# Expert stage by phases: a tile's u dot products first, then its v rows gathered by token

## What is computed

```python
q = (hb @ w_q).reshape(PEER_BLOCK, PEER_HEADS, 2, PEER_QDIM // 2)
s = jnp.einsum('nhpd,pkd->nhpk', q, sub_keys)
s_half, i_half = lax.top_k(s, PEER_TOPK)
cand = (s_half[:, :, 0, :, None] + s_half[:, :, 1, None, :]).reshape(PEER_BLOCK, PEER_HEADS, PEER_TOPK * PEER_TOPK)
cid = (i_half[:, :, 0, :, None] * PEER_NKEYS + i_half[:, :, 1, None, :]).reshape(cand.shape)
best_s, best_j = lax.top_k(cand, PEER_TOPK)
eid = jnp.take_along_axis(cid, best_j, axis=-1)
gate = jax.nn.softmax(best_s, axis=-1)
act = jax.nn.gelu(jnp.einsum('nd,nhkd->nhk', hb, u_tab[eid]))
out = jnp.einsum('nhk,nhkd->nd', gate * act, v_tab[eid])
```

## Time and profile before

| | us |
|---|---|
| median of 3 runs | 3094.18 |
| the runs | 3093.94, 3094.18, 3095.62 |
| span of the profiled execution, first to last instruction | 3089.7 |
| busy: PE, PEld | 2489.5, 1527.7 |
| busy: DVE, ACT, POOL | 1279.6, 386.2, 647.1 |
| expert stage, from the first gather's issue to the end | 1699.3 to 3089.7 |
| bytes read from HBM | 842.46 MB |
| of these gathers of POOL's queue | 586.10 MB |

### The profile page before, as it was taken

How to read it: one execution, slowest core, us unless ns; L and a number is a source line. 1 busy time by engine, 2 the same in 40 slices (tenths; PEclk the granted TensorE clock), 3 DMA queues, 4 the chain that set the end, 5 groups by cost and what they waited for, 6 DMA issues and landing times.

```text
span 3089.7 us, 33087 instructions
## 1 busy us (share of the span) xinstructions
PE 2489.5 (81%) x11463; PEld 1527.7 (49%) x11463; DVE 1279.6 (41%) x2256; ACT 386.2 (12%) x946; POOL 647.1 (21%) x736
## 2 busy tenths in 40 slices
PE   6888879999988688969997676777776777777776
PEld 5665658888877374338786222232322222222222
DVE  3213121003255562210147556555554555555554
ACT  1212120001131141110113000000000000000000
POOL 1000000000000123230000434344432343333332
PEclk9999999999988678979998998999999899999998
DMA  9999985444130263566420999999998799999997
GB/s 296 322 331 322 336 259 186 143 156 141 55 109 1 62 214 119 155 205 206 130 89 1 409 420 366 422 422 422 422 422 346 293 421 422 422 422 422 422 422 303
DMA packets 328937, 852.32 MB, mean 276 GB/s; under 512 B 21246, under 2 KB 232754, under 8 KB 260554
## 3 DMA queue, kind: packets, MB, share of 16 engines
q0 software_dynamic: 84000, 586.10, 46.7%
q1 hardware_dynamic: 240370, 259.48, 26.8%
q10 hardware_dynamic: 4476, 5.58, 0.6%
HBM read 842.46 MB, written 17.21 MB: 278 GB/s over the span
## 4 chain that ended last, share of the span: by engine, by line
PE 46%; DMA 28%; issue 10%; SPq 6%; DVE 5%; POOL 2%; ACT 2%; POOLq 0%; DVEq 0%; PEldq 0%; ACTq 0%
DMA sb_ring<-in_peer_u_dram,sb_work 24%; PE ps L539 12%; PE ps L2196 7%; DMA sb_ring<-in_w_ada_dram 4%; PE ps L1841 4%; PE ps L1730 4%; PE ps L1644 3%; PE ps L362 3%; SPq L200 2%; SPq L199 2%; PE ps L345 2%; POOL sb_ring L2066 2%; PE ps L1629 1%; PE ps L2216 1%; PE ps L1088 1%
## 5 line engine op out<-in xcount | busy, mean ns | idle before, releaser
L2196 PE MATMUL ps<-sb_ring,sb_levels 128*128 128x512 f32 x2048 | 956.5, 612 | 342.3 <-DVE sb_levels L2141 328.9
L2196 PEld LDWEIGHTS ps<-sb_ring,sb_levels 128*128 128x128 f32 x2048 | 375.1, 192 | 924.5 <-DVE sb_levels L2141 474.6
L2099 DVE SCALAR_TENSOR_TENSOR sb_pT<-sb_ring,sb_pT 128x2048 f32<-128x2048 f32 x256 | 586.8, 2292 | 502.2 <-DMA sb_ring<-in_peer_u_dram,sb_work 501.9
L2066 POOL DMA_INDIRECT sb_ring<-in_peer_v_dram,sb_work x256 | 252.2, 985 | 633.3 <-DVE sb_pT L2099 519.9
L539 PE MATMUL ps<-sb_hT,sb_ring 128*128 128x264 f32 x1664 | 370.8, 386 | 0.0
L539 PEld LDWEIGHTS ps<-sb_hT,sb_ring 128*128 128x128 f32 x1664 | 316.0, 190 | 54.4 <-issue 0.4
L2064 POOL DMA_INDIRECT sb_ring<-in_peer_u_dram,sb_work x256 | 270.2, 1055 | 136.7 <-issue 79.4
L2172 ACT ACTIVATE sb_small<-sb_small 128x1 f32<-128x1 f32 x256 | 51.9, 203 | 1224.0 <-DVE sb_pT L2099 1224.0
L987 POOL DMA_DIRECT2D out_conv_p_dram<-sb_work x1 | 0.7, 740 | 694.0 <-DVE sb_work L682 694.0
L345 PE MATMUL ps<-sb_ring,sb_work 128*32 128x256 f32 x1536 | 103.9, 416 | 27.5 <-DMA sb_ring<-in_w_ada_dram 27.5
L2141 DVE TENSOR_SCALAR sb_levels<-sb_ident,sb_small,sb_work 128x128 f32<-128x128 f32 x256 | 95.5, 373 | 69.5 <-ACT sb_small L2172 69.5
(11 more groups left out here) (533 smaller groups left out, 2308.9 us busy)
## 6 DMA issues: line engine op xcount, KB each, us to landing
sb_ring<-in_w_ada_dram SPq DMA_DIRECT2D x48, 2048.0 KB, 17.6
sb_ring<-in_w_in_dram SPq DMA_DIRECT2D x26, 2048.0 KB, 8.4
sb_ring<-in_cache_cmp_kv_dram SPq DMA_DIRECT2D x128, 256.0 KB, 3.3
sb_ring<-in_w_out_dram SPq DMA_DIRECT2D x8, 2048.0 KB, 9.8
sb_ring<-in_peer_wq_dram SPq DMA_DIRECT2D x8, 2048.0 KB, 8.3
sb_ring<-in_cache_sel_kv_dram SPq DMA_DIRECT2D x120, 128.0 KB, 2.9
sb_ring<-in_cache_sel_kv_dram POOLq DMA_DIRECT2D x116, 128.0 KB, 2.9
sb_ring<-in_state_win_kv_dram SPq DMA_DIRECT2D x4, 2048.0 KB, 22.7
```

The lines of the kernel that those rows point to most:

```text
L2066: pool.indirect_dma_start(vbuf[n0 % 4], None, io["peer_v"][0], bass.IndirectOffsetOnAxis(index, 0)).then_inc(v_in[n0 % 4], 16)
L2099: dve.scalar_tensor_tensor(products, ubuf[j], 1.0, h2, ALU.mult, ALU.mult, accum_out=dots[:, column:column + 1]).then_inc(sem("dot"), 1)
L2196: mm = pe.matmul(bank(bk + q), diag[:, n0 % 4, :], vbuf[n0 % 4][:, 512 * q:512 * q + 512], start=False, stop=False)
```

## The change

The expert stage is written anew; the picks are moved.

- **Order of gathers.** One list, `ENTRIES`, has all gathers: tile 0's 128 u gathers (one per slot), then its 128 v gathers (now one per token: the token's 128 slots on the partitions), then 8 u and 8 v gathers for the samples (u by head, v by head, with a sample's 16 slots of a head on 16 partitions), then tile 1's u and v. POOL walks the list without a loop.
- **Buffers.** All eight halves of the ring serve u and v in turn; a gather waits until the one that held its buffer has been used. The first 24 gathers use only four of them, in ring slots 0 and 1 of the four, and may begin while the query projection runs; the query weights use the other two slots only, head by head, so a load waits for the head two before it.
- **Picks head by head.** `dve_head` does one head of one tile to the end, the expert numbers included. In the query projection only tile 0's heads are picked, and after each head from the second on DVE does three dots of gathers that have been issued for the heads before. Key scores of a head are formed half a head earlier (after the first of the next head's two blocks). Tile 1's and the samples' picks follow in `dve_others`, after tile 0's last dot.
- **u phase.** The dots are done slot by slot as before, but in place (the product overwrites the row), with no gelu and no diagonal between them. After the last, ACT applies gelu to the 128 x 128 results at once and DVE multiplies with the gates.
- **v phase.** PE transposes the expert numbers (for the gathers) and the weights. For token n the weight column stands in a 128 x 32 block that is zero but for its own column (`wexp`: a cleared buffer in which ACT writes every 33rd column), and four products with 32 weight columns and 512 row columns put the four quarters of the token's sum on four groups of 32 partitions of one PSUM bank. 32 tokens fill a bank, two banks alternate, ACT moves them to rows (`whole`; for the last group DVE moves two of the four quarters). For the samples a head's 8 samples are one such product set, with `wexp_s`.
- **End of a tile.** The add, the norm and the scale are as before, but those of tile 0 and of the samples stand between tile 1's first dots; SP stores the results.

```diff
@@ sp_out
-            sp_project(sp, G_OUT + 8, 68, 8, io["peer_wq"][0], 0)
+            for h in range(HEADS):
+                sp.wait_ge(sem("proj_sum"), 8 + 52 + 2 * (4 + h + 1) if h < 2 else 8 + 68 + 2 * (h - 1))
+                sp.dma_start(ring[:, wq_slot(h), :].rearrange("p (k n) -> p k n", k=KD), item_src(io["peer_wq"][0], 256 * h)).then_inc(full[wq_slot(h)], 16)
...
+        ENTRIES = [("u", 0, n) for n in range(SLOTS)] + [("v", 0, n) for n in range(P)]
+        ENTRIES += [("u", NT, h) for h in range(HEADS)] + [("v", NT, h) for h in range(HEADS)]
+        ENTRIES += [("u", 1, n) for n in range(SLOTS)] + [("v", 1, n) for n in range(P)]
+        EARLY, PER_HEAD = 24, 3
+        NBUF = 2 * RING
+        rbuf = [ring[:, j // 2, (j % 2) * D:(j % 2 + 1) * D] for j in range(NBUF)]
+        buf_of = lambda e: e % 4 if e < EARLY else (e - EARLY + 4) % NBUF
...
@@ pe_queries
-                if h:
-                    scores(h - 1)
+                    if c == 0 and h:
+                        scores(h - 1)
                 rows(3 * h + 2)
...
@@ dve_queries
-            for h in range(HEADS):
-                dve.wait_ge(sem("keyscores"), h + 1)
-                best(P, range(NT), h, lambda t, half: ks[h % 2][:, t, half])
...
+            for h in range(HEADS):
+                dve.wait_ge(sem("keyscores"), h + 1)
+                dve_head(dve, P, 0, h, [ks0[h % 2][:, half] for half in range(2)])
+                if h:
+                    dve_dots(dve, 0, PER_HEAD * (h - 1), PER_HEAD * h)
+            dve_differences(dve, 0)
+
+        def dve_dots(dve, t, n0, n1):
+            for n in range(n0, n1):
+                rows, here, count = rows_at("u", t, n)
...
+                dve.wait_ge(here, count)
+                dve.scalar_tensor_tensor(rows, rows, 1.0, h2r[:, t, :] if t < NT else h2w, ALU.mult, ALU.mult,
+                                         accum_out=(dots if t < NT else dots_s)[:, n:n + 1]).then_inc(sem("dot"), 1)
...
+        def dve_experts(dve):
+            c = sem("dve_steps")
+            dve_dots(dve, 0, PER_HEAD * (HEADS - 1), 72)
+            dve_gates(dve, 0)
+            dve_ids(dve, 0)
+            dve_dots(dve, 0, 72, SLOTS)
+            dve_weights(dve, 0)
+            dve_others(dve)
+            dve_dots(dve, NT, 0, HEADS)
...
+            dve_add(dve, 0)
+            dve_dots(dve, 1, 0, 4)
+            dve_scale(dve, 0)
+            dve_dots(dve, 1, 4, 12)
+            dve_add(dve, NT)
+            dve_dots(dve, 1, 12, 16)
+            dve_scale(dve, NT)
+            dve_dots(dve, 1, 16, SLOTS)
+            dve_weights(dve, 1)
...
+        def pe_sums(pe, t, n0, n1):
+            for n in range(n0, n1):
...
+                w = wexp[G % 2][:, 32 * j:32 * j + 32] if t < NT else wexp_s[:, j, :]
+                pe.wait_ge(here, count)
+                for q in range(4):
+                    mm = pe.matmul(bank(G % 2)[32 * q:32 * q + 32, :], w, rows[:, 512 * q:512 * q + 512], start=j == 0, stop=j == last)
+                mm.then_inc(sem("v_used"), 1)
...
+        def pe_experts(pe):
+            pe_side(pe)
+            pe.wait_ge(sem("h2_wide"), 4)
+            pe_ids(pe, 0)
+            pe_weights(pe, 0)
+            pe_sums(pe, 0, 0, 44)
+            pe.wait_ge(sem("ids_ready"), 1)
+            pe_ids(pe, 1)
+            pe.wait_ge(sem("found_ready"), 1)
...
+            pe_sums(pe, 0, 44, P)
+            pe_sums(pe, NT, 0, HEADS)
+            pe_weights(pe, 1)
+            pe_sums(pe, 1, 0, P)
...
@@ pool_gather
-            pool.wait_ge(sem("proj_sum"), 8 + 84)
...
-                pool.wait_ge(sem("experts_ready"), t + 1)
...
+            pool.wait_ge(sem("proj_sum"), 8 + 68)
+            last = {}
+            for e, (kind, t, n) in enumerate(ENTRIES):
+                if e == EARLY:
+                    pool.wait_ge(sem("proj_sum"), 8 + 84)
...
+                b = buf_of(e)
+                if b in last:
+                    pool.wait_ge(sem("dot" if ENTRIES[last[b]][0] == "u" else "v_used"), done_of(last[b]))
+                last[b] = e
...
+                pool.indirect_dma_start(rbuf[b], None, io["peer_u" if kind == "u" else "peer_v"][0], bass.IndirectOffsetOnAxis(index, 0)
+                                        ).then_inc(row_in[b], 16)
```

More of the change, by code:

```diff
@@ L2036, in layer_program @@
-        vbuf = [ring[:, 2 + j // 2, (j % 2) * D:(j % 2 + 1) * D] for j in range(4)]
-        v_in = [sem(f"v_in{j}") for j in range(4)]
-        SEQ = (0, NT, 1)
-        FIRST = {0: 0, NT: SLOTS, 1: SLOTS + NB}
-        place = SEQ.index
-        def each_slot(eng, t, body, head=None, turns=(0, HEADS // 2)):
-            with eng.Fori(*turns) as i:
-                for half in range(2):
-                    if head:
-                        head(i, half)
-                    for s in range(TOPK):
-                        body(i, half, s, FIRST[t] + half * TOPK + s)
@@ L2247, in _ @@
             leave(sp, "sp_left")
-            for stage in (sp_w2, sp_states_stored, sp_samp, sp_out):
+            for stage in (sp_w2, sp_states_stored, sp_samp, sp_out, sp_results):
                 stage(sp)
```

567 lines of the change are left out of this document (289 added, 278 removed).

## The result

The changed kernel takes 2987.33 us (median of 4 runs, 2984.48 to 2987.95) against 3094.06 us for the kernel before (4 runs): ratio 0.9658, 95% interval 0.9642 to 0.9673, 107 us less. The forecast was 2972 us, range 2954 to 3035: the sign and most of the size are right, and 15 us of the gain are missing. The profiled execution has a span of 2985.6 us, where the sum made 2967.

The account below looks back on a forecast made before the run. Gathers from HBM were taken to bound the last 1390 us. Savings of 54.7, 21.8, 51 and 4.3 us less 10 make 122 us: span 2967, median forecast 2972 us, range 2954 to 3035.

Parts of the forecast that it names:

- Start of the stream: Query projection: 22 gathers leave the stream (54.7 us), which starts at 1677.5 and not at 1699.3 (21.8 us).
- No hole around the samples: Expert stage: eight buffers cover phase changes and tile 1's selection, so the 51 us lost inside the stage go.
- Dots against gather issue: U phases: DVE's dots hold back POOL's gathers, 2.52 us a row, a cost of 10 us.
- the loop: U phases with three gathers in flight: issue, landing and dot take 2.56 us a row.
- the shut-out by a pile: Start of tile 1's u phase: piled-up rows may keep POOL from issuing, 14 us once, counted in the range only.
- Tail: After the last byte: shorter PE work and fewer copies, 4.3 us less, 20.0 us in all.
- Sum: Whole span: start, latency, 506 transfers, 10 us for dots and the tail make 2967 us; 4.5 more for the median.
- the loop's term: U phases: the 10 us added to the stream for dots and gather issue delaying each other.
- The dots do not pace the u phases: Rival for the u phases: dots and POOL delay each other, 2.79 us a row, 71 us more, 3043; 13%.
- The projection did not stretch: Rival for the query projection: weight loads beside gathers exceed the pitch, 43 us more, 3015; 7%.
- Gathers by token: Rival for the v phases: gathering one token's 128 slots is slower, 129 us more, 3101; 7%.
- The early part works: Rival for the projection: experts or buffers ready only after it, 54.7 + 21.8 us gone, 3048; 3%.

Follow-up runs that it names:

- e2: Changed kernel with DVE's residual adds and final scales of tile 0 and the samples moved behind tile 1's last dot: 2984.2 us, ratio 0.9646 to the kernel before.
- e3: Changed kernel with tile 1's 128 dots taking the normalized rows from PSUM, so one operand in SBUF: 2979.1 us, ratio 0.9630 to the kernel before.
- e4: Changed kernel with no gather before the projection's last product and no dot between the heads: 3013.4 us, ratio 0.9743 to the kernel before.

## Why the prediction was right, and where it was short

**Start of the stream: right.** 22 gathers were to leave the stream and gather 22 to be out at 1677.5. It was out at 1682.88, and the same point ahead of the queries was 5.32 us later in this execution:

```profile
1514.64 0.14 POOL L2027 IOTA sb_work<- 128x16 f32 x1 [129.08 <-DVE sb_xT L1755]
```

```profile
1519.96 0.15 POOL L2247 IOTA sb_work<- 128x16 f32 x1 [128.66 <-DVE sb_xT L1761]
```

(the kernel before, then the changed one). Less that, it is 1677.56. A head's picks took 9.35 us (1570.71 to 1580.06), over the 8.7 to 8.9 of the sum, three dots 6.8 and not 6.9: 16.2 of the pitch of 16.45. That is why the mechanism held although a head is 0.5 us longer; the agreement to a tenth is luck, as head 6 also began 0.5 us earlier than forecast. The 5.3 us arise in stages that the edit leaves as they are: at POOL's operation at 1098.81 us the changed kernel's trace is 8.8 us late, and 3.4 of them come back by this mark. All twelve traces of kernels with the new stage have this mark later than the old one, between 1516.06 and 1526.35; whether that is more than the spread of executions is open, since there is one trace of before, and its span lies some 3 us below that of its median run, by the 1.6 to 1.7 us that lie between time and span in the later runs.

**No hole around the samples: right.** 422 GB/s from 2260 to 2330; the 51 us went. A token's row takes PE 1.07 us at the full clock, as in the earlier trace rows, and 1.94 at the granted clock of 0.50 (1.2 GHz), not 1.66:

```profile
2944.56 1.07 PE L2221 MATMUL ps<-sb_ring,sb_xT 128*32 128x512 f32 x8 [0.69 <-DMA sb_ring<-in_peer_v_dram,sb_above]
2947.04 1.94 PE L2221 MATMUL ps<-sb_ring,sb_xT 128*32 128x512 f32 x8 [1.42 <-DMA sb_ring<-in_peer_v_dram,sb_above]
```

Both are below 2.485 us, so PE waits for rows in the v phases at either clock.

**Dots against gather issue: the step that failed.** I took +10 us, 2.52 us for each of 234 rows (which makes 8 us, (2.52 - 2.485) x 234, and not 10), on the ground that a held gather delays DVE by 0.23 us. The hold is real, its price is none: in the steady u phase every gather is held for 2.18 us and leaves every 2.485 (gathers 108 to 128, 1900.57 to 1950.27), since DVE waits 0.2 us for its row anyway. What costs is the hold where something else is short. With two or three gathers in flight, the loop that I wrote as (0.8 + 4.6 + 2.29) / 3 = 2.56 has 5.4 us of landing in place of 4.6 (gather 24 out at 1687.71, its row read at 1693.12). With it the loop is 2.83; measured were 45 rows at 2.73, 10.9 us, as three gathers in that stretch were not held. And the shut-out by a pile, which stood in the range as "14 us once", came once: DVE's adds and scales were 14 us of work and not 9.7, the gather was out for 15.2 us, and it cost 9.1 us by its window, 7 by e2 and e3. Together 18 to 20 us for 10. I had the eight buffers as cover from gather 24 on, and did not ask when POOL could fill them: while one gather leaves per dot and is held, the number in flight does not grow.

**Tail: nearly right.** The last bytes land at about 2964.8 (0.39 of the 2 us from 2964 on), the span ends 20.8 us later; 20.0 were forecast.

**Sum.** 2967 + 5.3 + 0.8 is 2973; the stream itself was to end at 2942.4 without the loop's term (1682.9 + 2.1 + 506 x 2.485) and ended at 2964.8, so 22.4 us and not 10: 2985.5 against 2985.6. Of the 22.4, 18 to 20 are the two places; about 1.5 may be the v phases at 421 and not 422 GB/s, an estimate from their 630 us; the rest is not accounted for. From span to median I added 4.5 us, where 1.7 lie between them here (2987.33 - 2985.6). The 4.5 were not what a run takes besides its span: the profiled execution of the kernel before was a shorter one than its median run. So 18.6 us of span are 15.3 us of the forecast 2972, and this second error hides 3 us of what the sum of the span missed.

**The rivals.** The dots do not pace the u phases at 2.79 us: the first 45 rows take 2.73, for want of gathers in flight, and the rest 2.485, with every gather held. The projection did not stretch. Gathers by token run at 421 GB/s. The early part works, but my price for losing it, 76 us, was three times too high (23 to 26, e4): I charged it with the start at 1699.3, which the picks by head move by themselves.

## What to carry to other kernels

When a stream limited by transfers is fed by an engine that the consumer can hold up, ask how many transfers are in flight where the stream begins and after each pause, not only how many buffers there are: free buffers help only if the issuer gets a gap to fill them. Keep other work of the consumer out of the stretch in which it is level with the stream, and put it where it waits for another phase. And price an early start against the earliest start that the rest of the change allows, not against the old one.
